# One decoder trunk kernel: two weight loads and two row loads moved behind the next layer's modulation tiles, and the modulation vectors stored and reloaded from ScalarE's queue

## The reference, cut to what matters

```python
cond = silu(c)
for l in range(2):
    mod = (cond @ w_ada[l] + b_ada[l])[:, None, :]
    sh1, sc1, g1, sh2, sc2, g2 = jnp.split(mod, 6, axis=-1)
    h = x * (1.0 + sc1) + sh1
    u, q_lat, kv_lat, k_rope = jnp.split(h @ w_in[l], split_cols, axis=-1)
    pooled = causal_pool_mixer(u, w_pool[l], pool_scale[l])
    attn = mla_mixer(q_lat, kv_lat, k_rope, positions, ...)      # 6 heads of 128
    mixed = jnp.concatenate([pooled, attn], axis=-1) @ w_out[l]
    x = layer_norm(ALPHA * x + g1 * mixed, ln1_g[l], ln1_b[l])
    h = x * (1.0 + sc2) + sh2
    ffn = swiglu(h, w_sh_gate[l], w_sh_up[l], w_sh_down[l]) + routed_moe(h, ...)  # 64 experts, top 8
    x = layer_norm(ALPHA * x + g2 * ffn, ln2_g[l], ln2_b[l])
```

## Time and profile before

| | |
|---|---|
| median of three runs | 1310.39 us |
| span of the profiled execution | 1307.3 us |
| TensorE busy | 1232.3 us, 94% of the span |
| VectorE busy | 492.9 us, 38% |
| ScalarE busy | 249.9 us, 19% |
| GpSimd busy | 160.7 us, 12% |
| HBM read | 492.60 MB, 378 GB/s over the span |
| share of the 16 DMA engines, SyncE's loads (q1) | 92.7% |

### The profile page before, as it was taken

One profiled execution on the slowest core, in us unless ns is written; L12 is line 12 of the kernel. 1 busy time (PEld: TensorE's weight loads), 2 busy tenths in 40 slices (PEclk: granted clock), 3 DMA queues, 4 the chain that ended last, 5 costly groups with the idle time before them and its releaser, 6 DMA issues.

```text
span 1307.3 us, 28115 instructions
## 1 busy us (share of the span) xinstructions
PE 1232.3 (94%) x9342; PEld 771.9 (59%) x9342; DVE 492.9 (38%) x1111; ACT 249.9 (19%) x518; POOL 160.7 (12%) x587
## 2 busy tenths in 40 slices
PE   6999999999799999999988999999979999999995
PEld 3474566666466665566546557666646665566563
DVE  5666843222232222233347445222322322133335
ACT  1222211111111111111223312111111111111113
POOL 1000022111011111111000001111111111011110
PEclk9999999999899999999989999999999999899998
DMA  9999979999999999999867956999999999989992
GB/s 316 392 410 399 405 292 421 420 421 421 421 421 420 421 422 420 391 394 406 345 258 288 361 214 234 421 377 422 421 421 420 421 421 421 421 364 392 394 408 104
DMA packets 83921, 494.87 MB, mean 379 GB/s; under 512 B 11970, under 2 KB 20194, under 8 KB 29058
## 3 DMA queue, kind: packets, MB, share of 16 engines
q1 hardware_dynamic: 83842, 493.71, 92.7%
HBM read 492.60 MB, written 1.08 MB: 378 GB/s over the span
## 4 chain that ended last, share of the span: by engine, by line
PE 88%; DVE 4%; DMA 3%; issue 3%; SPq 2%; ACT 1%; DVEq 0%; ACTq 0%
PE ps L1028 32%; PE ps L1050 16%; PE ps L959 9%; PE ps L1071 8%; PE ps L969 5%; PE ps L688 3%; PE ps L881 3%; PE ps L909 2%; DMA w<-in_w_ada 2%; SPq L502 1%; PE ps L810 1%; PE ps L1000 1%; PE ps L1043 1%; PE ps L975 1%; DMA ring<-in_w_ada 1%
## 5 line engine op out<-in xcount | busy, mean ns | idle before, releaser
L1028 PE MATMUL ps<-ring,w 128*64 128x256 f32 (+1 forms) x3648 | 413.3, 385 | 0.5
L1028 PEld LDWEIGHTS ps<-ring,w 128*64 128x64 f32 (+1 forms) x3648 | 259.0, 127 | 68.6 <-issue 14.2
L1050 PE MATMUL ps<-ring,w 128*64 128x512 f32 (+1 forms) x912 | 207.7, 597 | 0.0
L1028 PE MATMUL ps<-flex,w 128*32 128x256 f32 x736 | 170.3, 391 | 26.5 <-issue 26.4
L1028 PE MATMUL ps<-w 128*32 128x256 f32 x736 | 170.8, 392 | 0.0
L1683 DVE SCALAR_TENSOR_TENSOR w<-ps,w 128x256 f32<-128x256 f32 x57 | 27.6, 484 | 374.1 <-PE ps L1028 374.1
L959 PE MATMUL ps<-hx,scat 128*128 128x512 f32 x472 | 138.3, 417 | 0.7 <-issue 0.7
L1669 DVE CAST scat<-ps 128x512 fp32r<-128x512 f32 x114 | 78.9, 692 | 158.9 <-PE ps L1050 158.9
L1028 PEld LDWEIGHTS ps<-flex,w 128*32 128x32 f32 x736 | 81.3, 113 | 84.7 <-issue 42.4
L1208 ACT ACTIVATE w<-ps 128x512 f32<-128x512 f32 x118 | 70.6, 598 | 290.4 <-PE ps L959 290.4
L1071 PE MATMUL ps<-scat 128*128 128x512 f32 x456 | 119.2, 403 | 0.0
(11 more groups left out here) (260 smaller groups left out, 1262.9 us busy)
## 6 DMA issues: line engine op xcount, KB each, us to landing
ring<-in_w_exp_gate SPq DMA_DIRECT2D x88, 1024.0 KB, 19.2
ring<-in_w_exp_up SPq DMA_DIRECT2D x88, 1024.0 KB, 22.3
ring<-in_w_exp_down SPq DMA_DIRECT2D x88, 1024.0 KB, 22.0
ring<-in_w_ada SPq DMA_DIRECT2D x30, 1024.0 KB, 10.9
w<-in_w_exp_gate SPq DMA_DIRECT2D x20, 1024.0 KB, 17.4
w<-in_w_exp_up SPq DMA_DIRECT2D x20, 1024.0 KB, 19.5
flex<-in_w_exp_gate SPq DMA_DIRECT2D x20, 1024.0 KB, 14.5
flex<-in_w_exp_up SPq DMA_DIRECT2D x20, 1024.0 KB, 16.1
```

Source lines behind the costliest of these rows:

```text
L1028: last = mm(ps[unit * g:unit * g + unit, bank, 0:F], hTb[:, kt, unit * g:unit * g + unit], weights(k)[:, kt, :], start=kt == 0, stop=kt == ...
L1050: last = mm(ps[unit * g:unit * g + unit, bank, :], midT[:, f, unit * g:unit * g + unit], down_w(k)[:, f, half * 512:(half + 1) * 512], sta ...
```

## The change

- In layer 1 the early loads of expert 1 (gate and up, 2 MB) no longer stand before `next_tiles`; they are issued with expert 0's, behind the shared expert. In layer 2 they stay where they were.
- The two norm rows (`ln1_g`, `ln1_b`, 512 KB each) are issued behind `next_tiles` in layer 1, and behind the early loads of expert 1 in layer 2, in place of ahead of the last four part 2 tiles.
- The stores of the modulation values, the wait for them, and the reload of gate row and columns are issued by ScalarE, after its last copy of an attention head and before its first norm. The gate row gets a semaphore of its own, `gate_row_in`; VectorE waits for the norm rows only ahead of `norm_x`.
- `next_tiles` issues all eight tiles in a row, and VectorE sums four before the first norm and four between the norms.

```diff
@@ SyncE
-                row(lng_row, lay(ln1_g, l), s["rows1_in"])
-                row(lnb_row, lay(ln1_b, l), s["rows1_in"])
...
                 ada_tiles(l, 2, (4, 5, 6, 7))
-                for half in range(2):
-                    load_gate_up(l, half, (1,), (1,))
+                if l:
+                    for half in range(2):
+                        load_gate_up(l, half, (1,), (1,))
                 sp.wait_ge(s["scores_done"], (l + 1) * H)
                 if l == 0:
                     sp.wait_ge(s["acc0_zeroed"], 2)
                     sp.dma_start(acc0[0:1, :], b_ada[1:2, 0:ADA_W]).then_inc(s["acc0_bias_in"], 16)
-                    next_tiles((0, 1, 2, 3))
-                store_mod(l, 1)
-                store_mod(l, 2)
-                if l == 0:
-                    next_tiles((4,))
-                sp.wait_ge(s["mod_written"], (l + 1) * 32)
-                mod_row(g_row, 2, s["rows1_in"])
-                for dst, m in ((sc2_col, 4), (sh2_col, 3)):
-                    sp.dma_start(dst, mod_dram[ds(l, 1), m * D:(m + 1) * D].rearrange("a (p k) -> p (a k)", k=KT)).then_inc(s["cols_in"], 16)
-                if l == 0:
-                    next_tiles((5, 6, 7))
+                    next_tiles(range(KT))
+                row(lng_row, lay(ln1_g, l), s["rows1_in"])
+                row(lnb_row, lay(ln1_b, l), s["rows1_in"])
                 sp.wait_ge(s["pv_ready"], (l + 1) * H)
...
                 for half in range(2):
                     load_gate_up(l, half, (0,), (0,))
+                    if l == 0:
+                        load_gate_up(l, half, (1,), (1,))
@@ ScalarE
                 mixed(H - 1)
+                for part in (1, 2):
+                    act.wait_ge(s["mod_val_ready"], l * 2 + part)
+                    dst = mod_dram[l:l + 1, part * ADA_W:(part + 1) * ADA_W].rearrange("a (g n) -> (a g) n", g=4)
+                    act.dma_start(dst, mod_val[part][0:P:32, :]).then_inc(s["mod_written"], 16)
+                act.wait_ge(s["mod_written"], (l + 1) * 32)
+                act.dma_start(g_row, mod_dram[l:l + 1, 2 * D:3 * D].to_broadcast([P, D])).then_inc(s["gate_row_in"], 16)
+                for dst, m in ((sc2_col, 4), (sh2_col, 3)):
+                    act.dma_start(dst, mod_dram[l:l + 1, m * D:(m + 1) * D].rearrange("a (p k) -> p (a k)", k=KT)).then_inc(s["cols_in"], 16)
@@ VectorE
-                    next_part(range(5))
+                    next_part(range(4))
...
-                dve.wait_ge(s["rows1_in"], (l + 1) * 48)
+                dve.wait_ge(s["gate_row_in"], (l + 1) * 16)
                 norm_stats(0, s["mix_done"])
                 normalise(0, l * 2 * NT + 1).then_inc(s["t_ready"], 1)
                 if l == 0:
-                    next_part((5, 6, 7))
+                    next_part((4, 5, 6, 7))
...
                 dve.wait_ge(s["t_ready"], (l + 1) * NT)
+                dve.wait_ge(s["rows1_in"], (l + 1) * 32)
                 norm_x(0)
```

More of the change, by code:

```diff
@@ L374, in decoder_trunk @@
         out_done ang_ready hi_ready place_ready order_done rc_ready ident_ready gates_split hi_copied hx_ready G_ready
-        gT_done dve_link waits_passed dist_ready""".split()
+        gT_done dve_link gate_row_in waits_passed dist_ready""".split()
         s = {n: sem(n) for n in names}
@@ L442, in ada_bias @@
                 sp.dma_start(mod_bias[part][0:P:32, :], src.rearrange("a (g n) -> (a g) n", g=4)).then_inc(s["bias_in"], 16)
[L444 to L448, removed]
             def lay(w, l):
```

## The result

The changed kernel takes 1320.75 us (median of four runs, 1319.37 to 1321.55) against 1309.81 us for the kernel before (now four runs): 0.8% slower, ratio 1.0076 with an interval of 1.0063 to 1.0088. I had forecast 1307.4 us. The profiled span went from 1307.3 to 1318.6 us.

The account below looks back on a forecast made before the run. A chain of computation before the expert weight stream starts at 174 us was taken as the bound; 0.57 + 2.17 + 0.28 = 3.0 us saved gave 1310.4 to 1307.4 us, range 1306.2 to 1308.6, wider range 1305.0 to 1311.0.

Parts of the forecast that it names:

- Loads taken from before the tiles: Layer 1 queue: 7.5 us less ahead of next-layer tiles, 2.5 us less ahead of the last four part 2 tiles.
- attention of layer 1: TensorE before the projection: earlier part 2 tiles cover waits of 0.79 and 0.22 us; gain 0.57 us.
- Four sums ahead of the norm: VectorE, layer 1: sums end at about 121.8; TensorE's 2.17 us wait goes, and transposes behind work save 0.28 us.
- the whole sum: All gains together: 0.57 + 2.17 + 0.28 = 3.0 us, median 1310.4 to 1307.4 us.
- the longer sum: Four sums between layer 1's norms: cover 1.2 us; if the first norm slips more, it costs one for one.
- Store and reload on ScalarE: ScalarE before layer 1's first norm: five issues cost nothing themselves; the norm can use the gate row up to 128.
- the low end: Layer 1 reload on ScalarE: stores 1.2 us, row 5.1 us, landing at about 121.5, cost 0.
- The rule of turns: DMA engines take turns, packet by packet, between queues with work; by it the row lands at about 122.
- Layer 2: Gain zero: TensorE waits for no tile; gate row 1 or 2 us later, still ahead of the projection's second piece.
- The slower one: Layer 1 gate row waits in one line behind SyncE's loads: 9.9 us slower, 1320.3 us; chance 0.09, 0.08 beyond 2.6 us.
- Slow stores by themselves: Layer 1 stores on ScalarE's queue again take 10.6 us, norm starts at 130.0: 1310.8 us, no change; chance 0.04.
- Gain given back in the stream: Weight stream starts no earlier because the queue is still full of later preloads: 1309.5 to 1310.4 us; chance 0.14.

Follow-up runs that it names:

- experiment 1: Changed kernel with store and reload back on SyncE in both layers, moved loads and sums of 4 and 4 kept: 1307.4 us, ratio 0.9975.
- experiment 4: Changed kernel, but in layer 2 SyncE issues shared expert and later experts only after gate row and columns land: 1313.51 us, ratio 1.0022.
- experiment 8: Changed kernel with store/reload on SyncE, sums 5 and 3, two filler matmuls for six in layer 1, experts 1 and 2 preloaded earlier: 1304.93 us, ratio 0.9956.
- experiment 3: Kernel before the change with only store and reload moved to ScalarE in both layers: 1323.38 us, ratio 1.0104.
- experiment 5: Changed kernel with two more unread 4 KB column loads on ScalarE's queue in layer 2: 1322.58 us, ratio 1.0091.
- experiment 2: Changed kernel with store and reload issued by SyncE again in layer 2 only: 1313.64 us, ratio 1.0025.
- experiment 6: Changed kernel with VectorE's sums split 5 and 3 again: 1321.56 us, ratio 1.0078.

## Why the prediction was wrong

*Loads taken from before the tiles; attention of layer 1.* Right: 0.57 us forecast, 17.47 to 16.90 us measured.

*Four sums ahead of the norm.* The sums ended at 121.95 for 121.8. "The norm now waits for something else, the second piece of the projection" was wrong in the changed kernel and right in experiment 1, where the whole sum came true: 3.0 us forecast, 2.96 us at the router, ratio 0.9975. That the longer sum costs time once the first norm slips was right too: TensorE waited 1.45 us before it summed over the partitions.

*Store and reload on ScalarE: the step that failed.* "I take the low end ... cost 0." Three things in it were wrong. It priced the gate row alone, while VectorE waits for the columns too. It shared the bandwidth by bytes ("half the rate for 512 KB"), where the engines share by packets (200 to 206). The rule of turns that it quotes was right, but it was not worked out in packets: 8 KB in 256 packets of columns took 5.9 us, 512 KB in 128 packets of the row 4.3. And it read 1.2 us for the store and 5.1 us for the row off stretches in which SyncE was holding its loads back or the reload stood ahead of them in one line; the change removed that very hold. Measured: the row takes 8.2 us in layer 1, where 5.1 and at most 2.5 more were taken, and the last column lands at 131.5, ten us later than the 121.5 that it had for the row.

*Layer 2.* "Zero" was the largest miss, 8.49 us: no tile is waited for, as I wrote, but the reload there now runs beside the loads of shared expert and experts 0 and 1, which SyncE issues at once. "The gate row comes 1 or 2 us later" had assumed an empty queue; experiment 4 made it empty, and the loss was gone.

*The rivals.* The slower one gave 1320.3 us and 1320.75 us was measured, but that is luck: its mechanism is not what happened. It had ScalarE's transfers wait in one line behind SyncE's, 9.9 us in layer 1 alone. The trace shows two lines that take turns, 2.8 us in layer 1 and 8.5 us in layer 2; in layer 2 the columns, issued at 756, land at 769, ahead of loads that SyncE had issued by 753 and that landed at about 771. What held of it is the arithmetic behind the norm: it said 21.5 us from the norm's start to the second transposes, and they began 21.7 us after it (132.03 to 153.75). The chance of 0.08 for slower was too small, since the low end was taken from rows of one queue, with no row of two loaded ones. Slow stores by themselves: the two stores end 4.5 us after their issue in layer 1 (114.5 to 119.05) and 4.9 in layer 2, but 2.0 us in experiment 4, so more than half of it was the other queue, and nowhere did they take 10.6 us. The prediction named beside this rival what the Trainium skill ("DMA: Bandwidth & Descriptors", section "Anatomy of one DMA") says on write receipts; that section describes transfers issued by GpSimd, and these are issued by SyncE and ScalarE. Gain given back in the stream: excluded by experiment 1, whose 2.96 us at the router are 3.3 us at the end by the ratio, and by experiment 8.

*The clock.* No step of the prediction had it. 3.05 of the 8.49 us in layer 2 are matmuls at a lower granted clock after the wait.

## What to carry to other kernels

A second queue was no fast lane here: while the first was loaded, each packet of the second waited for one of the first's, and its first packet came 3.2 to 3.6 us after the issue. So count the packets of what you move, not its bytes, and keep vectors of 32 bytes a partition off a queue that runs beside 8 KB packets: in the loaded queue itself the same columns landed in 4.0 us. Before an engine's wait is taken away, look at what the engine did not issue while it waited; that hold may be what made the next transfers fast. And a stall on TensorE is priced with the slower matmuls behind it.

## What the runs showed of the hardware

Two queues with work at once were served packet for packet, 200 to 206 and 274 to 275 in 5 us. A column vector of 4 KB, issued right behind the row of 512 KB in each case, took 2.9 us beside an empty queue, 11.9 us beside a loaded one, and 4.0 us within a loaded one. The first packet on ScalarE's queue started 1.0 us after the issue beside an empty queue and 3.2 to 3.6 us after it beside a loaded one; why, these runs do not show.

After waits of TensorE of 5.44 us in layer 2, and of 4.08 and 4.16 us in layer 1 (experiments 4 and 3), the granted clock was down, and the fourth piece of the projection took 8.8 to 9.0 us. After waits between 3.49 and 3.76 us in layer 1 it took 7.64, 8.73, 8.37 and 7.03 us (experiments 5, 2 and 6, and the changed kernel): the clock was down for part of it, or not at all. After 2.17 us, before the change, it took 7.03 us. What decides between these I did not find.
